# Softmax units of two stacked transformer blocks: logarithms of multiplicities in the mask, maximum and sum in the exponential, division by a diagonal matmul

## What is computed

```
for window, dil in ((128, 1), (512, 4), (2048, 16)):
    s = where(valid, einsum(q, k[gathered]) * scale, -inf)
    m = max(s);  p = exp(s - m);  den = sum(p)
    o = einsum(p, v[gathered]) / den;   lse = m + log(den)
o = sum over patterns of softmax(lse) * o
```

## Time and profile before

| | us |
|---|---|
| three runs | 2940.08, 2940.7, 2943.61 |
| median | 2940.7 |
| the profiled execution | 2945.13 |
| its span, first to last instruction | 2943.4 |
| matmuls busy (PE) | 2677.2 |
| VectorE (DVE) busy | 2073.5 |
| ScalarE (ACT) busy | 1564.6 |
| GpSimd (POOL) busy | 222.4 |

### The profile page before, as it was taken

How to read it: one execution, slowest core, us unless ns; L and a number is a source line. 1 busy time by engine, 2 the same in 40 slices (tenths; PEclk the granted TensorE clock), 3 DMA queues, 4 the chain that set the end, 5 groups by cost and what they waited for, 6 DMA issues and landing times.

```text
span 2943.4 us, 50303 instructions
## 1 busy us (share of the span) xinstructions
PE 2677.2 (91%) x19214; PEld 2508.7 (85%) x19214; DVE 2073.5 (70%) x2782; ACT 1564.6 (53%) x2102; POOL 222.4 (8%) x259
## 2 busy tenths in 40 slices
PE   6599986899998999899999999976999999977999
PEld 6499976899998999899998899954899899945999
DVE  4468755798988888788987787454677777453654
ACT  4343343677876777677776434453433434453432
POOL 2201030000000000000000010022011010022000
PEclk9699986999999999999999999966999999965999
DMA  6247641698988898889888575510487585510442
GB/s 253 88 180 300 241 151 43 246 335 320 350 314 312 314 349 322 308 324 338 335 335 325 211 300 205 193 64 27 167 304 288 208 305 203 189 54 1 148 174 100
DMA packets 76653, 678.77 MB, mean 231 GB/s; under 512 B 8624, under 2 KB 8752, under 8 KB 27696
## 3 DMA queue, kind: packets, MB, share of 16 engines
q1 hardware_dynamic: 55296, 599.10, 55.0%
q0 software_dynamic: 21168, 77.08, 6.5%
HBM read 675.10 MB, written 1.05 MB: 230 GB/s over the span
## 4 chain that ended last, share of the span: by engine, by line
PE 79%; DVE 9%; issue 4%; ACT 4%; POOL 2%; DMA 1%; DVEq 0%; SPq 0%; POOLq 0%; ACTq 0%
PE ps L1465 21%; PE ps L1466 21%; PE ps L1467 20%; PE ps L1875 9%; DMA ring<-wstream 1%; PE ps L1486 1%; DVE w_parts L1231 1%; PE ps L1842 1%; ACT w_parts L775 1%; PE ps L1884 1%; PE ps L1636 1%; DVE a_lo L1238 1%; PE ps L1850 1%; ACT w_parts L584 1%; DVE w_parts L976 1%
## 5 line engine op out<-in xcount | busy, mean ns | idle before, releaser
L1465 PE MATMUL ps<-a_hi,w_parts 128*128 128x256 f32 x2544 | 737.0, 290 | 66.0 <-DVE a_lo L932 24.2
L1466 PE MATMUL ps<-a_lo,w_parts 128*128 128x256 f32 x2544 | 734.2, 289 | 0.0
L1467 PE MATMUL ps<-a_hi,w_parts 128*128 128x256 f32 x2544 | 733.3, 288 | 0.0
L1231 DVE TENSOR_TENSOR w_parts<-ring,w_parts 128x1024 fp32r<-128x1024 f32 x448 | 548.1, 1224 | 73.5 <-ACT w_parts L775 71.7
L1465 PEld LDWEIGHTS ps<-a_hi,w_parts 128*128 128x128 f32 x2544 | 503.0, 198 | 74.0 <-issue 61.3
L1465 PE MATMUL ps<-w_parts 128*128 128x256 f32 x1792 | 530.3, 296 | 15.7 <-issue 15.6
L1466 PE MATMUL ps<-w_parts 128*128 128x256 f32 x1792 | 507.6, 283 | 0.0
L1467 PE MATMUL ps<-w_parts 128*128 128x256 f32 x1792 | 507.3, 283 | 0.0
L1466 PEld LDWEIGHTS ps<-a_lo,w_parts 128*128 128x128 f32 x2544 | 503.3, 198 | 0.0
L1467 PEld LDWEIGHTS ps<-a_hi,w_parts 128*128 128x128 f32 x2544 | 503.0, 198 | 0.0
L775 ACT ACTIVATE w_parts<-ring 128x1024 fp32r<-128x1024 f32 x448 | 472.3, 1055 | 3.6 <-DMA ring<-wstream 3.5
(11 more groups left out here) (225 smaller groups left out, 4185.0 us busy)
## 6 DMA issues: line engine op xcount, KB each, us to landing
ring<-wstream SPq DMA_DIRECT2D x378, 1536.0 KB, 8.0
proj<-astream POOLq DMA_DIRECT2D x144, 512.0 KB, 5.8
cst<-consts SPq DMA_DIRECT2D x1, 1700.0 KB, 8.6
vtok<-crow POOLq DMA_DIRECT2D x3, 512.0 KB, 4.0
xT<-x_in SPq DMA_DIRECT2D x1, 1024.0 KB, 5.0
out<-xT SPq DMA_DIRECT2D x1, 1024.0 KB, 3.9
proj<-wpool SPq DMA_DIRECT2D x1, 512.0 KB, 9.3
vec<-vectors SPq DMA_DIRECT2D x1, 136.5 KB, 2.2
```

The costliest lines, as they stand in the source:

```text
L1231: nc.vector.tensor_tensor(up_lo[:, n % 2, at], ring[:, s, at], up_hi[:, n % 2, at], ALU.subtract).then_inc(xup_lo, 1)
L1465: mm(o, stationary[0], moving[0], start=start, stop=False, skip_group_check=True)
L1466: mm(o, stationary[0], moving[1], start=False, stop=False, skip_group_check=True)
L1467: return mm(o, stationary[1], moving[0], start=False, stop=stop, skip_group_check=True)
```

## The change

The multiplicities enter the mask as logarithms (`lmult0`, `lmult1` in place of `mult0`, `mult1`; a key that counts zero times gets -1e30). VectorE's maximum is negated and is the bias of four exponentials on ScalarE, one for each head, each of which also writes the sum of its row. VectorE takes the reciprocals of the four sums and multiplies the identity with them into four diagonal 128 x 128 tiles, `rden`. In `values` a matmul by such a diagonal takes the place of the transpose: it turns and divides at once. GpSimd has no part in the softmax any more. The tile `rden(m)` lies in `proj` blocks 0 to 3 for m < 2 and in `branch` otherwise.

```diff
+        def rden(m):
+            room = proj[:, 0:4, :].rearrange("p k t -> p (k t)") if m < 2 else branch[:, KB * T:KB * T + 8 * P]
+            return room.rearrange("p (b h c) -> p b h c", b=2, h=4)
...
-            def softmax_units(m):                                    (GpSimd)
-                for i in range(5):
-                    if i < 4:
-                        u, nk = 4 * m + i, P * (i % 2 + 1)
-                        pool.wait_ge(max_ready, u + 1)
-                        at = 16 * (u % 2)
-                        nc.gpsimd.tensor_tensor(sm2[u % 2][:, :, 0:nk], sm2[u % 2][:, :, 0:nk],
-                                                small[:, at:at + 4].unsqueeze(2).broadcast_to([P, 4, nk]),
-                                                ALU.subtract).then_inc(sub_ready, 1)
-                    if i > 0:
...
-                        pool.wait_ge(rden_ready, u + 1)
...
-                                                ALU.mult).then_inc(p_ready, 1)
...
                         u, nk = 4 * m + i, P * (i % 2 + 1)           (ScalarE)
-                        act.wait_ge(sub_ready, u + 1)
-                        nc.scalar.activation(sm2[u % 2][:, :, 0:nk], sm2[u % 2][:, :, 0:nk], ACT.Exp)\
-                            .then_inc(exp_ready, 1)
+                        act.wait_ge(max_ready, u + 1)
+                        at = 16 * (u % 2)
+                        for h in range(4):
+                            nc.scalar.activation(sm2[u % 2][:, h, 0:nk], sm2[u % 2][:, h, 0:nk], ACT.Exp,
+                                                 bias=small[:, at + h:at + h + 1],
+                                                 accum_out=small[:, at + 4 + h:at + 5 + h]).then_inc(exp_ready, 1)
...
-                        nc.vector.tensor_reduce(small[:, at:at + 4], buf[:, :, 0:nk], AX, ALU.max)\
+                        nc.vector.tensor_reduce(small[:, at:at + 4], buf[:, :, 0:nk], AX, ALU.max, negate=True)\
                             .then_inc(max_ready, 1)
...
-                        dve.wait_ge(exp_ready, u + 1)
-                        if mults:
-                            after(dve, "dve", nc.vector.tensor_tensor(
-                                buf[:, :, 0:nk], buf[:, :, 0:nk],
-                                mults[(i - 1) % 2].unsqueeze(1).broadcast_to([P, 4, nk]), ALU.mult))
-                        after(dve, "dve", nc.vector.tensor_reduce(small[:, at + 4:at + 8], buf[:, :, 0:nk],
-                                                                  AX, ALU.add))
-                        nc.vector.reciprocal(small[:, at + 8:at + 12], small[:, at + 4:at + 8])\
-                            .then_inc(rden_ready, 1)
+                        dve.wait_ge(exp_ready, 4 * (u + 1))
+                        after(dve, "dve", nc.vector.reciprocal(small[:, at + 8:at + 12], small[:, at + 4:at + 8]))
+                        nc.vector.tensor_tensor(
+                            rden(m)[:, u % 2, :, :], C("ident").unsqueeze(1).broadcast_to([P, 4, P]),
+                            small[:, at + 8:at + 12].unsqueeze(2).broadcast_to([P, 4, P]), ALU.mult)\
+                            .then_inc(p_ready, 1)
...
-                        ins = nc.tensor.transpose(ps[:, 2 + i // 2, at:at + P],
-                                                  sm2[u % 2][:, i, kt * P:(kt + 1) * P], C("ident"))
+                        ins = mm(ps[:, 2 + i // 2, at:at + P], sm2[u % 2][:, i, kt * P:(kt + 1) * P],
+                                 rden(u // 4)[:, u % 2, i, :], start=True, stop=True)
...
-        put(f"mult{tt}", sum(((d >= 0) & (d <= w) & (d % s == 0)).astype(np.float32)
-                             for w, s in ((128, 1), (512, 4), (2048, 16))))
+        many = sum(((d >= 0) & (d <= w) & (d % s == 0)).astype(np.float32)
+                   for w, s in ((128, 1), (512, 4), (2048, 16)))
+        put(f"lmult{tt}", np.where(many > 0, np.log(np.maximum(many, 1.0)), NEG))
```

More of the change, by code:

```diff
@@ L77 @@
                ("cmask0", P), ("cmask1", T),
-               ("mult0", P), ("mult1", T), ("strict", T + P), ("cos", T), ("sin", T),
+               ("lmult0", P), ("lmult1", T), ("strict", T + P), ("cos", T), ("sin", T),
                ("invcnt", 4 * 16), ("iota", NE), ("slots", CAP)):
@@ L505, in _ @@
             windows(0)
-            softmax_units(0)
             pool.wait_ge(as_ready, KB * (SPLIT_INPUTS.index("c0") + 1))
@@ L510, in _ @@
             windows(1)
-            softmax_units(1)
             pool.wait_ge(x_ready, KB * 4)
@@ L516, in _ @@
             sticks(2)
-            softmax_units(2)
             pool.wait_ge(as_ready, KB * (SPLIT_INPUTS.index("c2") + 1))
@@ L523, in _ @@
             sticks(3)
-            softmax_units(3)
         @block.scalar
@@ L998, in residual, with softmax_units @@
                     ins.then_inc(x_ready, 1)
-            def softmax_units(m, masks, mults, meanwhile=None):
+            def softmax_units(m, masks, meanwhile=None):
                 for i in range(5):
@@ L1018, in softmax_units @@
                     if i > 0:
-                        u, nk, buf = 4 * m + i - 1, P * ((i - 1) % 2 + 1), sm2[(i - 1) % 2]
+                        u = 4 * m + i - 1
                         at = 16 * (u % 2)
-                        dve.wait_ge(exp_ready, u + 1)
-                        if mults:
-                            after(dve, "dve", nc.vector.tensor_tensor(
-                                buf[:, :, 0:nk], buf[:, :, 0:nk],
-                                mults[(i - 1) % 2].unsqueeze(1).broadcast_to([P, 4, nk]), ALU.mult))
-                        after(dve, "dve", nc.vector.tensor_reduce(small[:, at + 4:at + 8], buf[:, :, 0:nk],
-                                                                  AX, ALU.add))
-                        nc.vector.reciprocal(small[:, at + 8:at + 12], small[:, at + 4:at + 8])\
-                            .then_inc(rden_ready, 1)
+                        dve.wait_ge(exp_ready, 4 * (u + 1))
[4 more added lines that the diff above has]
+                            .then_inc(p_ready, 1)
                         if meanwhile and i < 4:
@@ L1071, in mixer1 @@
                 lo_tiles(IN_STAGE[m], range(2, STREAM[IN_STAGE[m]]))
-                softmax_units(m, [C(f"cmask{i % 2}") for i in range(4)], (C("mult0"), C("mult1")),
-                              lambda i: lo_outproj(m, i // 2, i % 2))
+                softmax_units(m, [C(f"lmult{i % 2}") for i in range(4)], lambda i: lo_outproj(m, i // 2, i % 2))
                 cat_norm(m)
@@ L1161, in mixer2 @@
                                                                      ALU.add, ALU.add))
-                softmax_units(m, [C("cmask0"), C("cmask1"), select[0][:, :], select[1]], None)
+                softmax_units(m, [C("cmask0"), C("cmask1"), select[0][:, :], select[1]])
                 cat_norm(m)
```

7 lines of the change are left out of this document (removed).

## The result

The changed kernel took 2904.64 us in the median of four runs (2898.63 to 2907.64), the kernel before 2940.39 us beside it: ratio 0.9869, 95% interval 0.9856 to 0.9882, that is 35.8 us faster. Forecast were 2919.7 us with a range from 2905 to 2936. The sign and the place were right, the size was not: the first rival, a clock at 2.4 GHz through most of the four sections, had been priced at 2905 and given one chance in ten. One execution of a later kernel (the copy cut in two) took 5658.85 us in a slow state, and no comparison here uses it.

The account below looks back on a forecast made before the run. Chains of hand-offs in four softmax sections, mostly at 1.2 GHz, were taken to bound the kernel. With a partly risen clock, -16 us (first two) and -5 (last two) sum to -21 from 2940.7: 2919.7 us, range 2905 to 2936.

Parts of the forecast that it names:

- the first rival: Clock stays at 2.4 GHz through nearly all four softmax sections: about -36 us, 2905 us; chance 10%.
- Reading the profile: Four softmax sections, together 150.5 us, are chains of hand-offs with no engine full, nearly all at 1.2 GHz.
- The exponentials: ScalarE, per unit of four heads: four biased exponentials with sums replace one, 1.66 and 2.09 us against 0.63 and 1.06.
- The sum's price: ScalarE, the sum each exponential leaves behind: 0.08 us a head, between bounds of 0 and 0.2.
- The third rival: ScalarE's sixteen exponentials a section become the chain, kernel slower; at 0.6 us a head +4, 2944.7 us; chance 5%.
- The turn by a matmul: TensorE: four and eight full fp32 matmuls take 1.96 and 3.68 us at 1.2 GHz, 1.1 and 2.0 at 2.4.
- The replays: Sections at 1.2 and 2.4 GHz: first 6.4 or 14.0 us faster; fourth 1.9 slower or 8.4 faster.
- Which clock?: Clock rises once or twice per section and falls again: -8 each in the first two, -2 and -3 in the last two.
- somewhat over half of the way: Last two sections, place between the 1.2 and 2.4 GHz replays: -3 from (+1.9, -8.4), -2 from (+3.1, -7.2).
- The stated reason: TensorE in the sections: real matmuls fill gaps and its busy share is higher, so the clock rises.
- The Trainium skill's sentence: Transposes don't count as clock-gate activity as matmuls do; would speak for a higher clock after the change; no size given.
- Rival (d): GpSimd's saved time returns at the next stage, the norm behind the softmax; given nothing.

Follow-up runs that it names:

- the copy cut in two: Changed kernel with ScalarE's copy of the turned tile cut in two, the first half copied while TensorE turns the other two heads; 2907.16 us.
- fillers: Changed kernel plus five unused 512-column matmuls in each of the first two sections, where TensorE waits for the first diagonal; 2895.40 us.
- The exponential alone: Kernel before with logarithms in the mask and maximum and sum in ScalarE's exponentials; GpSimd still multiplies by 1/sum, turns stay transposes; 2915.01 us.

## Why the prediction was wrong in size

- **Reading the profile** was right in the main. The four sections are chains, a saving in them is a saving of the kernel, and the stages behind gave nothing back: from the first section to the second it is 300.0 us before and 298.3 and 298.6 after. "Nearly all of these stretches lie at 1.2 GHz" holds for the fourth alone: with two levels, clocks of 0.61, 0.61 and 0.65 mean that a fifth to a third of the others was at 2.4 GHz.
- **The exponentials** were right: 1.66 and 2.09 us for four forecast, 1.65 (86.45 to 88.10) and 2.06 us measured. The sum's price of 0.08 us, taken from VectorE's record, is 0.09: in the kernel without sums in the second block four exponentials take 1.26 and 1.71 us. The third rival, ScalarE as the bound, is out.
- **The turn by a matmul** was right: forecast 1.1 and 2.0 us at 2.4 GHz, measured 1.16 and 2.05. At 1.2 GHz 1.96 was forecast for four and 3.68 for eight; 2.08 us were measured in the first section, and 3.68 and 3.78 for eight in the kernel before with matmul turns.
- **The replays** were right where the clock was what they assumed. The fourth section at 2.4 GHz was to take 26.65 us (2664.85 to 2691.5); it took 26.50. The second at 2.4 GHz was to take 26.8 us; with fillers and the clock at 1.00 it took 27.4. The first was forecast at 40.8 - 8 = 32.8 us and took 33.1 and 32.3.
- **Which clock?** is the step that failed, for the last two sections. "Once or twice in each section and to fall again", -3 and -2 us, was wrong: the clock was up from the first turn to the end, or nearly (0.89), or up with falls between (0.80), and the fourth and third gained 8.5 and 7.3 us, in the second execution 6.3 and 5.0. I had weighed a stretch of the old chain, the one before the clock fell, in which TensorE was busy for 1.64 of 3.40 us and GpSimd for 2.50. The change removes that work of GpSimd, and with it a wait of 2.21 us; 0.21 us is left in its place. This term was mis-sized by 6 to 11 us together. -3 and -2 are also not "somewhat over half of the way" between the ends, but just under it. The second section gained 10.4 and 10.3 where 8 was forecast.
- **The stated reason** for a higher clock, gaps that close, is the one that the runs support: filling one gap raised it in the first two sections. It is not the whole rule, since the clock also fell in between in the repeat of the changed kernel, whose waits were no longer than in the first profile (1.13 us at most in the fourth section). The Trainium skill's sentence (TensorE: Matmul & The Clock Gate, Part 4: PE-mode transpose) had been named as a rule by which the matmuls would hold the clock. The exponential alone, with transposes, reached 0.90 and 0.89 in the last two sections. Its transposes ran at full clock, eight in 1.09 us against 1.97 at 1.2 GHz. Whether a transpose counts for less than a matmul of the same length no run here isolates; a matmul as turn was not needed for the high clock.
- **A term that was missing**, and a second step that failed: the pauses at the loop's turn, 15.6 us before and 7.0 or 9.1 after, so 6.5 to 8.6 us of the 35.8. Rival (d) gave nothing to other stages, and looked only at the stage right behind. What ties the pauses to the change is the count of TensorE's instructions ahead of the loop; why they follow it stays open. With sections of -30 to -34 and pauses of -6.5 to -8.6 the sum would be -37 to -43. The medians differ by 35.8 us in the first group and 42.4 in the second.
- **The range** ended at 2905 since I took the first rival at its price and added nothing beyond it. The sections alone, -34.0 and -30.1 us, would have stayed within it (2906.7 and 2910.6); the pauses carried the time out.

## What to carry to other kernels

When a chain of short hand-offs is thinned out, replay it at both clocks, and ask which of TensorE's waits the change takes away before you guess at the clock. By the replays all four sections at 1.2 GHz would have gained 7.8 us together; they gained 34.0 and 30.1, so more than 20 us are, by this estimate, the clock that came up when the waits went. A matmul in place of a cheaper instruction loses in the sections by itself (15 us here) and is worth it only for what it removes, so after a change that worked, take its parts out one at a time: the division could leave the second block altogether. Before a difference of a few us is put down to an edit, compare the stretches that the edit doesn't touch, and count what the edit puts ahead of a loop.

## What the runs showed of the hardware that I had not expected

- Five matmuls whose result nobody reads made two sections 6 to 7 us shorter (62.8 to 56.6 us against the second profile of the changed kernel, 63.5 against the first), by holding the clock at 0.94 and 1.00 through a wait of 4.6 us.
- At the turn of a long loop TensorE pauses for 3.4 to 8.2 us, and VectorE and ScalarE pause near it. In 23 of the 26 pauses the profile shows no releaser ("issue"); in the other three it names VectorE, which stood still itself. The length goes with the number of TensorE's instructions ahead of the loop, and not with what they do: the changed kernel and the same with transposes differ only in TensorE's turns and have 3.5 to 4.8 and 7.5 to 7.8 us. Instructions at the start of TensorE's list, far from the loop, moved it from 8 to 4.8 us in one kernel and from 3.4 to 6.1 in another. The likeliest reason is the place of the code, which is only argued: no run isolates it. After a pause of 8.1 us TensorE ran 4.8 us at 1.2 GHz; the clock had fallen within the pause.
- The same kernel has the same section at 26.5 and at 28.8 us in two executions, since the clock fell in between in one of them (third and fourth: granted 0.89 and 0.80). What remains open is why the cut copy, a shorter chain, had the lower clock in the second section (0.73 against 0.83 twice).
- A one-column fp32 matmul takes TensorE 0.21 us for each of its two records, from start to start, at full clock (88 records in 18.93 us). A 128-column one took 0.13 (16 records in 2.05 us).
